# A decoder step at full precision: the low halves of two weight pieces per group change, computed on POOL instead of on DVE

## The reference

```python
q_g, k_g, v_g, r_g, lr_g, q_a, k_a, v_a, gate_a, gate_b = jnp.split(h @ w_in, idx, axis=-1)
# gated linear attention (GLA), chunk by chunk, with a running state s
o_inter = jnp.einsum('nhid,nhde->nhie', qc * jnp.exp(b), s)
s_new = jnp.exp(b_last[:, :, 0, :])[..., None] * s + jnp.einsum('nhjd,nhje->nhde', kc * jnp.exp(b_last - b), vc)
# sliding-window attention with sinks: p = softmax(scores + bias), o = p @ v
y_g = gla_output(o_g, r_g, gla_norm_g)                       # RMS norm and silu(r)
merged = jax.nn.sigmoid(gate_a) * y_g + jax.nn.sigmoid(gate_b) * o_a
```

## Time and profile before

| what | value |
|---|---|
| median of 3 runs | 2072.45 us (2062.92 to 2074.95) |
| profiled execution, its time | 2069.95 us |
| its span in the trace | 2068.3 us |
| granted TensorE clock, mean | 0.926 of full speed |
| busy: PE / DVE / ACT / POOL | 86% / 57% / 39% / 15% |
| low halves of wide pieces on DVE (L1407) | 16 times, median 2293 ns |

### The profile page before, as it was taken

The page is one execution under the profiler, slowest core; times in us unless marked ns, Lnnn a source line. Parts: engine busy times, 40 slices in busy tenths (PEclk is TensorE's granted clock), DMA queues, the critical chain, the costliest instruction groups (busy, mean ns, idle before and its releaser), DMA issues.

```text
span 2068.3 us, 28515 instructions
## 1 busy us (share of the span) xinstructions
PE 1789.0 (86%) x8798; PEld 1452.7 (70%) x8798; DVE 1170.6 (57%) x1669; ACT 813.6 (39%) x1444; POOL 319.3 (15%) x390
## 2 busy tenths in 40 slices
PE   2999998898889889888987799519999999999965
PEld 2899997776677667677764688417777777777742
DVE  4411111666666656666765233476777777777726
ACT  2422221334333423433331122305666666666633
POOL 1200000212222222122210011130000000000025
PEclk9999998999899889989996699758999999999987
DMA  6396423224422432333237822636999999999944
GB/s 200 137 279 182 117 61 119 76 91 128 128 92 67 128 128 67 110 93 104 76 115 240 295 78 95 244 138 242 398 398 399 399 399 397 398 399 399 396 166 200
DMA packets 240649, 422.83 MB, mean 204 GB/s; under 512 B 24976, under 2 KB 123168, under 8 KB 240344
## 3 DMA queue, kind: packets, MB, share of 16 engines
q1 hardware_dynamic: 187120, 321.93, 44.0%
q0 software_dynamic: 20048, 69.06, 9.4%
q10 hardware_dynamic: 33408, 30.94, 4.3%
HBM read 354.83 MB, written 78.55 MB: 210 GB/s over the span
## 4 chain that ended last, share of the span: by engine, by line
PE 48%; issue 8%; DVE 5%; ACT 1%; POOL 1%; DMA 1%; POOLq 0%; DVEq 0%; SPq 0%; ACTq 0%
PE PS L1883 11%; PE PS L1884 11%; PE PS L1885 11%; PE PS L2190 5%; PE PS L1890 2%; PE PS L2046 1%; PE PS L2053 1%; PE PS L1979 1%; PE PS L2018 1%; PE PS L2017 1%; POOL hh L968 1%; DVE zz L1855 1%; PE PS L2076 1%; PE PS L1988 0%; DVE ya L1867 0%
## 5 line engine op out<-in xcount | busy, mean ns | idle before, releaser
L1750 DVE TENSOR_TENSOR wm_lo<-raw,wm_hi 128x2048 fp32r<-128x2048 f32 x156 | 352.0, 2289 | 147.3 <-ACT wm_hi L1280 147.3
L1280 ACT CAST wm_hi<-raw 128x2048 fp32r<-128x2048 f32 x160 | 301.6, 1907 | 75.1 <-PE PS L1885 75.1
L1883 PE MATMUL PS<-w_hi,hT_hl 128*128 128x512 f32 x560 | 239.2, 427 | 5.0 <-issue 5.0
L1884 PE MATMUL PS<-w_lo,hT_hl 128*128 128x512 f32 x560 | 231.5, 413 | 0.0
L1885 PE MATMUL PS<-w_hi,hT_hl 128*128 128x512 f32 x560 | 229.9, 411 | 0.0
L1883 PE MATMUL PS<-wm_hi,xT_hi 128*128 128x512 f32 x512 | 203.9, 398 | 3.1 <-DVE xT_lo L1815 3.1
L1885 PE MATMUL PS<-wm_hi,xT_lo 128*128 128x512 f32 x512 | 201.1, 393 | 0.0
L1884 PE MATMUL PS<-wm_lo,xT_hi 128*128 128x512 f32 x512 | 200.7, 392 | 0.0
L1923 PE MATMUL PS<-xa_hi,wn 128*128 128x384 f32 x480 | 161.8, 337 | 0.2 <-ACT ev L1075 0.2
L1924 PE MATMUL PS<-xa_lo,wn 128*128 128x384 f32 x480 | 161.1, 336 | 0.0
L1925 PE MATMUL PS<-xa_hi,wn 128*128 128x384 f32 x480 | 161.1, 336 | 0.0
(11 more groups left out here) (345 smaller groups left out, 3363.2 us busy)
## 6 DMA issues: line engine op xcount, KB each, us to landing
raw<-in_w_gate SPq DMA_DIRECT2D x64, 1024.0 KB, 8.7
raw<-in_w_up SPq DMA_DIRECT2D x64, 1024.0 KB, 9.7
raw<-in_w_down SPq DMA_DIRECT2D x64, 1024.0 KB, 10.1
hT_hl<-hl_dram POOLq DMA_DIRECT2D x70, 512.0 KB, 5.5
braw<-in_w_in SPq DMA_DIRECT2D x16, 1024.0 KB, 6.0
obuf_dram<-yb ACTq DMA_DIRECT2D x32, 512.0 KB, 6.9
nd_dram<-ev ACTq DMA_DIRECT2D x72, 192.0 KB, 2.4
nd<-nd_dram SPq DMA_DIRECT2D x36, 384.0 KB, 4.3
```

The costliest lines, as they stand in the source:

```text
L1280: act.copy(wm_hi[:, j], raw[:, j]).then_inc(m_hi[j // 4], 1)
L1750: dve.tensor_tensor(wm_lo[:, j], raw[:, j], BF(wm_hi[:, j]), ALU.subtract).then_inc(m_lo[j // 4], 1)
L1883: pe.matmul(out, x_hi, w_hi_, start=start, stop=False)
L1884: pe.matmul(out, x_hi, w_lo_, start=False, stop=False)
```

## The change

For the three group changes the subtraction of pieces 0 and 1 is taken out of DVE's step 7 and put on POOL, between its steps 7 and 8. It is the same operation on the same operands. Since two engines now raise `b_lo`, DVE's `wide` waits for the pieces ahead of its own. ACT's casts stay where they are.

```diff
@@ gpsimd @@
             step(n0 + 7, 7, s1_, (n0 + 7) // 2, False)
+            if g + 1 < G:
+                for j in range(2):
+                    pool.wait_ge(b_hi, upto((g + 1) * WIDE + j))
+                    c = slice(j * DV, (j + 1) * DV)
+                    t = half_slot(g + 1, j)
+                    pool.tensor_tensor(w_lo[t][:, :, c], braw[:, j], BF(w_hi[t][:, :, c]), ALU.subtract).then_inc(b_lo, 1)
             step(n0 + 8, 8, s0_, (n0 + 8) // 2, False)
@@ vector @@
         def wide(g, j):
             dve.wait_ge(b_hi, upto(g * WIDE + j))
+            dve.wait_ge(b_lo, upto(g * WIDE + j - 1))
@@ vector @@
-            step(n0 + 7, s1_, (n0 + 7) // 2, False, 0, (0, 1) if g + 1 < G else ())
+            step(n0 + 7, s1_, (n0 + 7) // 2, False, 0)
             step(n0 + 8, s0_, (n0 + 8) // 2, False, 0, (2,) if g + 1 < G else ())
```

## The result

The changed kernel takes 2090.93 us as the median of 4 runs (2088.57 to 2094.97), the kernel before 2070.67 us (4 runs). The ratio is 1.0104, with a 95% interval of 1.0068 to 1.0140: about 20 us slower (14 to 29), where the forecast was 2088.

A forecast was written before the change was run, and what follows sets the result against it. An ordinary step keeps PE busy 17.0 of 18.6 us; at group changes DVE's subtraction is on step 7's path. Losses of 5.7 + 5.1 + 4.9 = 15.7 on 2069.95 give 2085.7, plus 2.5 to the median: 2088, range 2069 to 2097.

The forecast's parts named there:

- The gain of step 7: Step 7: without the subtraction DVE's `Et` starts right behind ACT's, winning 2.98 of 4.49 us per change.
- Both subtractions of POOL ahead of `kk`: Start of step 8: POOL begins at 507.14, 0.36 us before `kk` is issued, and takes 4.50 us per subtraction.
- DVE waits for the port: Step 8: DVE operations with two SBUF inputs wait while POOL reads SBUF; net loss 5.7, 5.1 and 4.9 us.
- How the wait is shared out: Step 8: `kk` waits for the first subtraction until 511.64 and goes through; `qq` waits for the second until 516.35.
- PE at the low clock: Step 8: PE may return at 1.2 GHz, transposes up to 1.4 us late; nothing in the sum, 5 in the high end.
- The late load of piece 2: Step 8: SP's load goes out at 511.64, landing by 522.1 before ACT's cast at 522.7; costed at nothing.
- the rival's limit: Step 8, if DVE is not blocked: ACT's cast due at 514.05 waits 3.6 us for the load of piece 2.
- The free offload: Step 8: POOL's subtractions do not block DVE; best 8 us of gain, time 2064 to 2074; chance 0.10.
- One blocked: Step 8: only one of two subtractions blocks DVE, `nmx` 2.8 us later; 8 us slower, 2080; chance 0.12.
- the worse case: Step 8: blocked, plus PE's low clock or slower POOL subtractions; 21 to 25 us, 2094 to 2098; chance 0.17.
- The late start: Step 8: POOL starts up to 1 us later, `kk` and `qq` already through; 2079; chance 0.05.

The follow-up runs named there:

- after_gap: Changed kernel with POOL waiting for its first subtraction to end before starting the second; ratio 1.0077 against the kernel before.
- after_pos: Changed kernel with POOL's two subtractions held until DVE has issued `kk`, `qq`, `Sm` and the copy of `e` in step 8; ratio 1.0060 against the kernel before.
- memset_long: Changed kernel with POOL's subtractions replaced by repeated memsets, each waiting for the one before, about 4.5 us per piece intended; ratio 0.9973 against the kernel before.
- memset_short: Changed kernel with each POOL subtraction replaced by one memset per piece, which reads nothing; ratio 0.9980 against the kernel before.

## Why the prediction was right or wrong, point by point

- **The gain of step 7.** Reckoned 2.98 us per change; measured 2.6, 3.0 and 3.0. ACT's casts limit it, as said.
- **Both subtractions of POOL ahead of `kk`, at their natural length.** Reckoned to start 0.36 us ahead of `kk` and to take 4.50 us each; measured 0.33 us and 4.50 to 4.51 for all six. The gap in the output costs nothing.
- **DVE waits for the port.** Right in kind and in size. The changes of steps 7 and 8 together cost 5.9, 5.0 and 4.9 us, where 5.7, 5.1 and 4.9 were reckoned: 15.8 against 15.7. The memsets, beside which `kk` takes 0.29 us, show that this is the reading of POOL and not its lateness.
- **How the wait is shared out.** Wrong in detail. I let `kk` through between the two subtractions, as rows 8 show it for operations of other lines. There POOL waits between its instructions for the one before to end; here it doesn't, and `kk` waited for both. after_gap, with that wait, behaves as I had written except that `qq` slips through too and `Sm` pays. But the missing wait is not the whole reason, since in after_pos `mx` got through without it; that stays open. The sum is nearly the same either way: step 8 took 30.3 us and in after_gap 30.1.
- **PE at the low clock.** Taken as nothing in the sum, and rightly. Seven matmuls of the second wide product ran at the lower level and it ended at 531.6, just ahead of DVE's subtraction of piece 2 at 531.7.
- **The late load of piece 2.** ACT did not wait for it in the changed kernel. In memset_long, where DVE was not blocked, it waited for 3.0 us over the three changes: the rival's limit is real. The wait of 1.0 us per change is less than the 3.6 that I gave it, in part because the cast itself came 1.8 us later through the waits of `Sm` and `nmx`.
- **What was missing.** The output stores at the start of the next group. The prediction looked at all that the change makes later and not at what it makes earlier relative to its neighbours: the raw loads overtook the stores and cost 5.1 us at the first change. With that term, 0.7 us the other way in the other two steps 0 and 2.3 in all other steps, the traces give 17.9 us, and the timed runs say 20 (14 to 29). That the median came within 3 us of 2088 is in part luck: the stores were left out, the base of 2072.45 was 1.8 us above the median of 2070.67, and the two work against each other.
- **Rivals.** The free offload falls with 8.8 us of `kk`. Even had POOL not read, memset_short says the gain would have been 4 us (0 to 8), since `Sm` waits for a writer as well. "One blocked" falls too: `kk` waited for both subtractions. Of the two causes named for the worse case neither came about, as the points above show; what made it a little worse than forecast was a third one, the stores. The late start falls; after_pos shows what it would have given, 7.5 us less in the steps 8 than the change as made.

## What to carry to other kernels

Before moving an elementwise operation with operands in SBUF from DVE to POOL, list DVE's instructions in the time in which POOL will work: here each one with two inputs in SBUF, or a `tensor_scalar`, waited for POOL's instruction to end, however small it was, and all behind it waited too. 4.5 us taken off DVE bought 3 us per change and cost 8. Look first for idle time of the same engine a little earlier in the step: moving the casts by a few instructions gave 17 us without any other engine, and one piece per step and loads kept off the stores made it 22 to 26.

## What the runs showed of the hardware

- Two POOL subtractions back to back held a DVE instruction issued 0.33 us into the first for both, 8.79 us. With POOL waiting for the first to end the wait was 4.34 us, and two DVE instructions went through between them (after_gap). Without that wait, one issued 2.7 to 4.0 us into the first went through between them as well (after_pos).
- A POOL memset of 2048 columns takes 1.82 us and does not delay a DVE product of two SBUF operands (0.29 us), but it does delay a `tensor_scalar`, be it with two columns of scalars (2.95 us instead of 0.41, behind two memsets) or with a constant on four columns (1.16 instead of 0.16).
- POOL waited 1.8 to 2.6 us for three small output stores to land when no weight loads went out ahead of them, and 5.1 to 6.8 us when 2 MB of weight loads did.
